# Weight splits inside the gate's slices, and rotation tables made one layer ahead

## What is computed

```python
# first block, per layer
proj = rms_norm(h, g_mix) @ w_in            # q, k, v, xr, gr
o = diff_attention(partial_rope(q), partial_rope(k), v, lam)   # 4 heads, causal
y = rg_lru(causal_conv(xr)) * gelu(gr)
h = h + concat([o, y]) @ w_out
h = h + square(relu(rms_norm(h, g_mlp) @ w_mlp_in)) @ w_mlp_out
gate = sigmoid(rms_norm(h, g_ple) @ w_ple_gate)
h = h + gate * (p @ w_ple_proj)
# second block, per layer
h = rms_norm(x, g_pre_mix)
u, q, k, v, iq, ik, iw = split(h @ w_in)    # q, k, iq, ik are rotated (rope)
mix = concat([pool_mixer(u), top128_attention(q, k, v, iq, ik, iw)]) @ w_out
x = x + rms_norm(mix, g_post_mix)
x = x + rms_norm(square(relu(rms_norm(x, g_pre_ffn) @ w_ff1)) @ w_ff2, g_post_ffn)
```

## Time and profile before

| | before |
|---|---|
| time, 3 runs: median (lowest, highest) | 2562.69 (2561.21, 2563.07) |
| the profiled execution's own time | 2563.96 |
| its span | 2561.9 |
| TensorE busy | 2422.1 (95%) |
| VectorE / ScalarE / GpSimd busy | 1474.0 / 833.4 / 360.5 |
| mean granted clock of TensorE | 0.975 |

### The profile page before, as it was taken

How to read it: one execution, slowest core, us unless ns; L and a number is a source line. 1 busy time by engine, 2 the same in 40 slices (tenths; PEclk the granted TensorE clock), 3 DMA queues, 4 the chain that set the end, 5 groups by cost and what they waited for, 6 DMA issues and landing times.

```text
span 2561.9 us, 28886 instructions
## 1 busy us (share of the span) xinstructions
PE 2422.1 (95%) x11342; PEld 1942.7 (76%) x11350; DVE 1474.0 (58%) x2112; ACT 833.4 (33%) x1166; POOL 360.5 (14%) x281
## 2 busy tenths in 40 slices
PE   7999999999998999999897989999989888999996
PEld 6877888887786888888766767888866666788885
DVE  6765554455776644444669756435556965634543
ACT  4554222234546322223431443222232244322221
POOL 2002000001100100001227321000033632200002
PEclk9999999999999999999999989999989999999998
DMA  4311222222221222222211111222212111122221
GB/s 151 108 62 54 104 95 97 98 99 81 98 92 50 83 99 99 98 99 97 77 66 66 50 66 66 93 105 98 82 66 91 66 50 66 50 98 99 98 98 49
DMA packets 33017, 215.53 MB, mean 84 GB/s; under 512 B 4112, under 2 KB 4368, under 8 KB 7824
## 3 DMA queue, kind: packets, MB, share of 16 engines
q1 hardware_dynamic: 32912, 214.08, 23.3%
HBM read 211.97 MB, written 2.10 MB: 84 GB/s over the span
## 4 chain that ended last, share of the span: by engine, by line
PE 81%; DVE 10%; POOL 4%; ACT 3%; issue 2%; DMA 0%; POOLq 0%; ACTq 0%; SPq 0%; DVEq 0%
PE ps L356 74%; DVE wl L328 1%; ACT wh L321 1%; POOL wl L337 1%; DVE tmp L1792 1%; DVE hl L509 1%; POOL arena L1446 1%; PE ps L1921 1%; PE ps L1957 1%; PE ps L1981 1%; PE ps L1971 1%; PE ps L469 1%; PE ps L1191 1%; PE ps L493 1%; DVE gl L509 1%
## 5 line engine op out<-in xcount | busy, mean ns | idle before, releaser
L356 PE MATMUL ps<-gh,wh 128*128 128x512 f32 x1504 | 602.1, 400 | 39.0 <-DVE gl L509 15.5
L356 PE MATMUL ps<-hh,wh 128*128 128x512 f32 x1504 | 602.5, 401 | 32.4 <-issue 13.2
L356 PE MATMUL ps<-gh,wl 128*128 128x512 f32 x1504 | 591.0, 393 | 0.0
L356 PE MATMUL ps<-hh,wl 128*128 128x512 f32 x1504 | 590.8, 393 | 0.0
L356 PE MATMUL ps<-gl,wh 128*128 128x512 f32 x1504 | 590.8, 393 | 0.0
L356 PE MATMUL ps<-hl,wh 128*128 128x512 f32 x1504 | 590.7, 393 | 0.0
L328 DVE TENSOR_TENSOR wl<-wr,wh 128x2048 fp32r<-128x2048 f32 x176 | 406.2, 2308 | 275.1 <-ACT wh L321 275.1
L321 ACT ACTIVATE wh<-wr 128x2048 fp32r<-128x2048 f32 x196 | 374.1, 1909 | 553.9 <-PE ps L356 553.9
L356 PEld LDWEIGHTS ps<-gh,wh 128*128 128x128 f32 x1504 | 285.1, 190 | 112.9 <-issue 21.9
L356 PEld LDWEIGHTS ps<-hh,wh 128*128 128x128 f32 x1504 | 285.0, 190 | 109.3 <-issue 29.3
L356 PEld LDWEIGHTS ps<-hh,wl 128*128 128x128 f32 x1504 | 284.6, 189 | 61.8
(11 more groups left out here) (232 smaller groups left out, 2385.7 us busy)
## 6 DMA issues: line engine op xcount, KB each, us to landing
wr<-in_weights SPq DMA_DIRECT2D x196, 1024.0 KB, 4.8
x<-in_xt SPq DMA_DIRECT2D x4, 512.0 KB, 7.0
out_yt<-x SPq DMA_DIRECT2D x8, 256.0 KB, 2.0
tmp<-in_positions SPq DMA_DIRECT2D x4, 256.0 KB, 2.7
arena<-in_gates SPq DMA_DIRECT2D x2, 512.0 KB, 8.0
arena<-in_embed SPq DMA_DIRECT2D x2, 512.0 KB, 5.6
par<-in_params_b SPq DMA_DIRECT2D x2, 274.0 KB, 3.0
par<-in_params_a SPq DMA_DIRECT2D x2, 157.5 KB, 6.7
```

The costliest lines, as they stand in the source:

```text
L356: done = pe.matmul(out, stationary, moving, start=(first and n == 0), stop=(last and n == 2), skip_group_check=True)
```

## The change

1. In the gate tail of both first-stack layers the splits of the next chunks move from ahead of a pair of slices to inside a slice: on ScalarE behind the sigmoid of slice 0, 3 and 5, on VectorE behind the addition to x of the same slice.
2. The tables of both second-stack layers are made in the layer before. SP loads the positions into the arena once the sixteenth score of that layer's attention is out, ahead of the MLP's weight loads. VectorE makes the angles between the first and the second half of the last MLP block. ScalarE takes the sines behind that half's first chunk. The layer itself reads the finished tables and writes the products with its root to the old place.
3. In the second-stack layers the mask copy moves from the layer's start to the end of the top-128 search.

```diff
+SPLIT_AFTER_GATE = {0: A_GATE + 2, 3: A_GATE + 3}
+FOLLOWING_AFTER_GATE = 5
+NEXT_ANGLES, NEXT_TABLES = 2048, 3072
+def load_next_positions(sp, mem, sem, positions, steps):
+    sp.wait_ge(sem["scored"], steps)
+    sp.dma_start(mem.arena[:, NEXT_ANGLES:NEXT_ANGLES + S].bitcast(I32), positions).then_inc(sem["next_positioned"], 16)
+def next_angles(dve, steps, mem, sem):
+    dve.wait_ge(sem["next_positioned"], 16)
+    rotary_angles(dve, steps, mem, mem.arena[:, NEXT_ANGLES:NEXT_ANGLES + S], mem.arena[:, NEXT_ANGLES + S:NEXT_ANGLES + 2 * S])\
+        .then_inc(sem["next_tables"], 1)
+def next_sines(act, mem, sem):
+    whole, left = mem.arena[:, NEXT_ANGLES:NEXT_ANGLES + S], mem.arena[:, NEXT_ANGLES + S:NEXT_ANGLES + 2 * S]
+    act.wait_ge(sem["next_tables"], 1)
+    act.activation(mem.next_sin, left, ACT.Sin, scale=mem.cst[:, C_SIGN:C_SIGN + 1]).then_inc(sem["next_tables"], 1)
+    act.activation(mem.next_cos, whole, ACT.Sin, scale=-1.0, bias=mem.cst[:, C_HPI:C_HPI + 1]).then_inc(sem["next_tables"], 1)
...
 first stack, SP:
+        if following.second:
+            load_next_positions(sp, mem, sem, next_positions, STEPS)
         with sp.Fori(0, FB) as j:
...
 first stack, ScalarE:
             for t in range(2):
                 own_slice(2, 2 * (c - c0 - BC) + t, A_TILE[c] + t, par[:, AP_GPLE:AP_GPLE + KT])
+            if following.second and c == c0 + BC:
+                next_sines(act, mem, sem)
...
         for c in range(A_GATE, A_CHUNKS):
-            if c + 1 < A_CHUNKS:
-                if c > A_GATE:
-                    split_high(act, mem, sem, c + 1, a_used(c + 1))
-            else:
-                split_high(act, following.mem, following.sem, 0)
             for t in range(2):
                 n = 2 * (c - A_GATE) + t
                 act.wait_ge(sem["drained"], A_TILE[c] + t + 1)
                 act.activation(tmp[:, 1, :], tmp[:, 0, :], ACT.Sigmoid).then_inc(sem["gate_out"], 1)
+                if n in SPLIT_AFTER_GATE:
+                    split_high(act, mem, sem, SPLIT_AFTER_GATE[n], a_used(SPLIT_AFTER_GATE[n]))
+                if n == FOLLOWING_AFTER_GATE:
+                    split_high(act, following.mem, following.sem, 0)
                 act.wait_ge(sem["finished"], n + 1)
                 input_high(act, following, n)
...
 first stack, VectorE:
         mlp_first(c0, once, FB - 1)
+        if following.second:
+            next_angles(dve, own, mem, sem)
         for c in range(c0 + BC, A_GATE):
             split_low(dve, mem, sem, c + 1)
...
                 dve.tensor_tensor(x[:, n, :], x[:, n, :], tmp[:, 1, :], ALU.add).then_inc(sem["finished"], 1)
+                if n in SPLIT_AFTER_GATE:
+                    split_low(dve, mem, sem, SPLIT_AFTER_GATE[n])
+                if n == FOLLOWING_AFTER_GATE:
+                    split_low(dve, following.mem, following.sem, 0)
...
 second stack, SP (and the same load ahead of the MLP if a layer follows):
-        sp.dma_start(tmp[:, 0, :].bitcast(I32), positions).then_inc(sem["positioned"], 16)
...
 second stack, ScalarE:
-        act.wait_ge(sem["tables"], 1)
-        act.activation(sin, tmp[:, 1, :], ACT.Sin, scale=cst[:, C_SIGN:C_SIGN + 1]).then_inc(sem["turned_tables"], 1)
-        act.activation(cos, tmp[:, 0, :], ACT.Sin, scale=-1.0, bias=cst[:, C_HPI:C_HPI + 1]).then_inc(sem["turned_tables"], 1)
         split_high(act, mem, sem, 2, b_used(2))
...
         for c in range(c0 + BC, B_CHUNKS):
+            if following and c == c0 + BC + 1:
+                next_sines(act, mem, sem)
...
 second stack, VectorE:
-        dve.wait_ge(sem["positioned"], 16)
-        rotary_angles(dve, own, mem, tmp[:, 0, :], tmp[:, 1, :]).then_inc(sem["tables"], 1)
-        own.mark(dve.tensor_copy(mask[0], cst[:, C_CHUNK:C_CHUNK + P]))
...
-        dve.wait_ge(sem["turned_tables"], 2)
-        own.mark(dve.tensor_tensor(sin, sin, mem.rb[:, :], ALU.mult))
-        own.mark(dve.tensor_tensor(cos, cos, mem.rb[:, :], ALU.mult))
+        dve.wait_ge(stage.before.sem["next_tables"], 3)
+        own.mark(dve.tensor_tensor(sin, mem.next_sin, mem.rb[:, :], ALU.mult))
+        own.mark(dve.tensor_tensor(cos, mem.next_cos, mem.rb[:, :], ALU.mult))
...
         picks(TOPK // 8 - rounds[0])
+        own.mark(dve.tensor_copy(mask[0], cst[:, C_CHUNK:C_CHUNK + P]))
...
         mlp_first(B_CHUNKS - 2 * BC, once, FB - 1)
+        if following:
+            next_angles(dve, own, mem, sem)
         mlp_second(B_CHUNKS - 2 * BC, once)
```

More of the change, by code:

```diff
@@ L124, in __init__ @@
         self.praw = arena[:, A1_CR:A1_CR + 2 * S]
+        self.next_cos, self.next_sin = (arena[:, NEXT_TABLES + S * n:NEXT_TABLES + S * (n + 1)] for n in range(2))
 def build(nc, weights, params_a, params_b, gains, gates, embed, constants, positions, xt, out):
@@ L152, in build @@
             if n < DEPTH:
-                programs.append(first_stack_layer(stage, n, weights, params_a, gains, gates, embed, constants, xt, positions[0:P, :]))
+                programs.append(first_stack_layer(stage, n, weights, params_a, gains, gates, embed, constants, xt,
+                                                  positions[0:P, :], positions[P:2 * P, :]))
             else:
@@ L191 @@
     "o_mean o_root o_normed o_back o_high o_low embed_high embed_low hidden hidden_high hidden_low gate_in gate_out padded "
-    "finished "
+    "finished next_positioned next_tables "
 )
 B_NAMES = (
-    "loaded0 loaded1 next_gains vectors positioned high low product drained squared gathered summed mean root diag spread "
-    "kept gain_high gain_low own tables turned_tables weights_turned masked swapped rotated logit rectified weighed "
+    "loaded0 loaded1 next_gains vectors high low product drained squared gathered summed mean root diag spread "
+    "kept gain_high gain_low own weights_turned masked swapped rotated logit rectified weighed "
     "pooled_ready pool_product pool_high pool_low scored maxed exped scaled_done turned untangled weighted pair_high pair_low "
     "updated branch_scaled added zeroed hidden hidden_high hidden_low padded pool_own finished folded raw_squared "
-    "raw_gathered raw_summed raw_mean raw_root raw_diag raw_spread raw_kept renewed "
+    "raw_gathered raw_summed raw_mean raw_root raw_diag raw_spread raw_kept renewed next_positioned next_tables "
 )
@@ L585, in a_used, with first_stack_layer @@
     return A_TILE[c - 1]
-def first_stack_layer(stage, layer, weights, params, gains, gates, embed, constants, xt, positions):
+NEXT_ANGLES, NEXT_TABLES = 2048, 3072
[11 more added lines that the diff above has]
+    act.activation(mem.next_cos, whole, ACT.Sin, scale=-1.0, bias=mem.cst[:, C_HPI:C_HPI + 1]).then_inc(sem["next_tables"], 1)
+def first_stack_layer(stage, layer, weights, params, gains, gates, embed, constants, xt, positions, next_positions):
     mem, sem, following, shared = stage.mem, stage.sem, stage.following, stage.shared
@@ L1132, in program_dve @@
         for c in range(A_GATE, A_CHUNKS):
-            if c + 1 < A_CHUNKS:
-                if c > A_GATE:
-                    split_low(dve, mem, sem, c + 1)
-            else:
-                split_low(dve, following.mem, following.sem, 0)
             for t in range(2):
@@ L1398, in program_sp @@
             load_gains(sp, mem, sem, gains, DEPTH + layer + 1)
+            load_next_positions(sp, mem, sem, positions, STEPS)
         with sp.Fori(0, FB) as j:
```

## The result

The changed kernel takes 2543.28 us (median of 4 runs, 2541.06 to 2544.82); the kernel before, run beside it on the same chip, took 2561.95 (4 runs, 2559.49 to 2563.07). The ratio is 0.9932, 95% interval 0.992 to 0.9945: 0.7% faster. A later set of runs of the changed kernel gave 2539.86 and 0.9926 (0.9914 to 0.9937). The profiled execution has a span of 2539.9 us at a mean granted clock of 0.979; before it was 2561.9 at 0.975.

A forecast was written before the change was run, and what follows sets the result against it. TensorE, busy 95% of the span, bounds the kernel, losing time to gate-tail and second-stack stalls and low clock. 4.5 + 8.4 − 0.3 + 4.9 = 17.5 us saved gives 2545.2 us, range 2541 to 2554.

The forecast's parts named there:

- Gate of layer 0, 4.5: Layer 0's gate tail: third chunk's split comes in time, saving 2.8 us of stall and 1.6 to 1.7 of clock.
- Gate of layer 1, 8.4: Layer 1's gate tail: ScalarE-VectorE-GpSimd chain walked slice by slice, about 1 us per GpSimd delay; second stack's second chunk 8.4 us earlier.
- rival 2: Layer 1's gate: no GpSimd delay, tail saves 10.3, low clock behind first sums (1.6) goes; total 21.0, 2541.7 us; chance 0.12.
- Rival 1: Gate tail: each GpSimd pair holds VectorE for all its 2.6 us; total saved 10, time 2552.7 us; chance 0.16.
- the lost clock behind the 4.1 us stall included: Layer 1's gate: the 8.4 us saved was said to contain the clock lost behind the 4.1 us stall.
- MLP tail, -0.3: Layer 1's last MLP block: added angle work delays the weight split, so TensorE waits 0.3 us; ends 0 and 2.5 for sines.
- Second stack, first layer, 0: Start of the second stack's first layer: the tables give TensorE nothing; the 1.09 us drained-bank wait stays.
- Second layer, 3.3 + 1.6: Second stack's second layer start: drained bank 3.3 us earlier, plus 1.6 us of low clock counted as saved (ends 0 and 1.6).
- Rival 3: Tables give 0.5 us: second layer keeps its low clock, MLP tail stalls 0.3 and 2.5; total 13.4, 2549.3 us; chance 0.10.
- Rival 4: MLP starts: weight loads starve behind SP's new wait, making the kernel slower, 2575 us at 35 us lateness; chance 0.03.
- VectorE adds of 1.5 us and more in most slices: Sign for layer 1's gate: VectorE's adds would take 1.5 us or more in most slices.
- the drained bank's wait: Sign at the start of the second stack's second layer: TensorE's 2.71 us wait for the drained bank falls to near 1.3.

The follow-up runs named there:

- experiment 4: Changed kernel with the third gate chunk's split put back to its old place, behind slice 1, in layer 0 alone; 2547.4 us, once.
- experiment 5: Changed kernel with GpSimd's second addition of each pair in the gate cut to 8 columns; 2539.22 us, ratio 0.9914 to the kernel before.
- Experiment 7: Changed kernel with the angle work done twice in the MLP tail of the first stack's last layer; 2548.06 us, once.
- experiment 8: Changed kernel with the folded layer's weight split ahead of its spread, and layer 1's angles behind the next weight split, sines one chunk later; 2539.14 us, ratio 0.9913.
- experiment 1: Kernel before with only the gate tail's splits moved, tables made in the layer itself as before; 2544.6 us, ratio 0.994.
- experiment 3: The changed kernel again, unaltered, timed beside the kernel before; 2539.86 us, ratio 0.9926.
- experiment 6: Changed kernel with the fourth gate chunk's split one slice earlier, behind slice 2's sigmoid, in both layers; 2539.73 us, ratio 0.9918.
- experiment 9: Changed kernel with the fourth gate chunk's split one slice earlier, the folded layer's split ahead of its spread, and angles and sines later; 2539.14 us, ratio 0.9918.
- experiment 2: Changed kernel with the old gate order, so only the tables' half of the change; 2557.39 us, ratio 0.9987 to the kernel before.

## Why the prediction was right, and where it was not

The forecast was 2545.2, 17.5 us saved. The ratio of 0.9932 on 2562 is 17.4 us (14.1 to 20.5), the second set's 0.9926 is 19.0 (16.1 to 22.0). The mechanism was right for the order of the work and wrong in part for the clock. That the total agrees to 0.1 us with the first set is luck: the terms below miss by 0.9 up to 1.6 down, and the clock gave on average some us that no term has. By its own steps:

- **Gate of layer 0, 4.5.** Right: experiment 4 gives 4.50, with its 2.8 us of stall and the clock back at 0.86. Missed was the chunk of the next layer, 0.86 more. The prediction looked only at whether that split would be in time after the change, not at the 0.56 that it had cost before.
- **Gate of layer 1, 8.4.** The walk held: from the first sigmoid to the second stack's second split 41.7 us (1216.22 to 1257.94) where 41.1 was predicted, brackets of 0.79 and 0.64 where 0.8 and 0.7 were. The second chunk starts 49.41 us behind the root copy (1262.72 less 1213.31), where it was 57.06 (1277.59 less 1220.53): 7.65 saved. Of the 0.75 too much, 0.6 is in the chain itself: by ScalarE's rows the two slices in which GpSimd's pair falls on the multiply took 5.30 and 5.28 where 5.1 was taken, and the other steps are each 0.1 or less over. The rest is TensorE's way from the last k-slice to the second chunk, 4.98 where 4.9 was taken, and rounding. GpSimd's delay was the right term: experiment 5 takes the second additions out, and what rival 2 says of the order then happens (no bracket, sums 2.5 us earlier; the prediction has 10.3 less 8.4, 1.9, for it). Rival 2's other half, the low clock behind the first sums, came in the first profile of after and stayed away in the second (60.37 and 58.76 in the table). Rival 1's full 2.6 us per pair did not come; the last section shows why.
- **The clock in layer 1's gate.** One part of my reasoning was wrong without changing the sum: "the lost clock behind the 4.1 us stall included". The two profiles of before have a granted clock of 0.57 and of 0.79 from 1234 to 1242. The run with the higher clock got through the chunk sooner, waited 0.92 for the next one instead, and both came to the second stack's first chunk 42.57 us behind the root copy (1263.10 less 1220.53, 1262.04 less 1219.47). What the one run lost more by the low clock cost it nothing, since the chain, not TensorE, set the pace.
- **MLP tail, -0.3.** The sign and place right, the size 0.42, the slower restart included. Experiment 7 shows that there is no cover. The relus behind a sigmoid cost nothing, since no other stretch grew.
- **Second stack, first layer, 0.** Right: 0.79 and 1.07 stay (in the changed kernel at 1274.43 and 1279.39), and experiment 8 shows what they wait for.
- **Second layer, 3.3 + 1.6.** The order of the work gave 3.83: from the chunk before (1919.62, with its bracket of 0.18) to the one behind the drained bank it was 19.57, and is 15.74 (1904.65 to 1920.39). Of the 0.5 more, 0.2 lies ahead of the multiplication of the sine by the root (now at 1917.48) and 0.3 behind it, in the rotation, where the 3.3 had assumed no change. The weak step is the clock: "I count the 1.6 as saved". Of the three profiles that have the 2.7 bracket, two have a low clock behind it (0.86 and 0.75 in 12 us) and one has 1.00; of the ten with 0.81 none has a low clock there. So the 1.6 is no fixed part of the wait's price, and the tables alone did not lower the clock's loss on average (below).

By the order of the work the change is worth 5.36 + 7.65 - 0.42 + 3.83 = 16.4 us (with the 1.7 of clock in layer 0's gate, which came every time). That is 1.1 less than the forecast: 0.9 and 0.5 more than the terms for layer 0 and the second layer, 0.75 and 0.1 less for layer 1's gate and MLP, and 1.6 less for the clock. The first pair of profiles shows 22.0. The rest is the clock, 1.6 in layer 1's attention and 3.2 in the second stack's second attention (5.09 less the 1.9 of the drained bank), and 0.6 ahead of the first root copy, which comes at 38.66 and 38.03 (and at 38.80 in the second profile of after, so that this too differs from run to run).

Whether the new order also loses less to the clock can be read from the granted clock that is on record for every run. The share of the clock that was not granted, times the span, averaged over the runs of a kernel (all of one set; the standard deviation over a kernel's runs is 4 to 7 us):

| kernel | runs | mean time | span times share not granted |
|---|---|---|---|
| before | 16 | 2560.0 | 56.0 |
| gate edit alone | 6 | 2545.0 | 49.6 |
| tables alone | 11 | 2557.0 | 56.9 |
| after | 6 | 2540.8 | 49.1 |

Over the three sets, 32 runs of the kernel before average 56.7, and 30 runs of the six kernels with the new gate order (experiments 1, 3, 5, 6, 8 and 9) average 48.7. The gate edit lowers the loss, the tables don't. Part of the 8 us is known: 1.7 is layer 0's gate, already in the 5.36, and 1.7 to 3.4 was lost behind the 4.10, where it cost no time. What is left shows in the mean times. They are 2.0 us better than the 12.95 for the gate edit, and 2.8 better than the 16.4 for the changed kernel; by the same estimate experiments 5, 6, 8 and 9 are 2.7 to 4.7 better than their order of the work says, and the tables alone are 0.5 worse. So low-clock stretches also came less often with the new gate order, worth some 2 to 5 us for which the prediction had no term. By what steps, so far behind the gate, no run here shows.

Rival 3 (the tables give 0.5 us) lies just outside experiment 2's interval of 1.0 to 5.9, and the sixth line of the table and the 0.42 in the MLP tail, where it has 2.8, speak against it. Rival 4 (weight loads starve) is refuted by MLP stretches that changed by nothing but the 0.42. Among the signs, the "VectorE adds of 1.5 us and more in most slices" came in four of eight, and the drained bank's wait is 0.81 where 1.3 was forecast.

## What to carry to other kernels

Where three engines in turn work on each slice, walk their chain from end to end before counting TensorE's brackets one by one: it tells whether a bracket is a loss of its own or only the place where a slow chain is waited for. Moving one split then shifts the bracket, and only work taken off the chain (here GpSimd's additions) shortens it. And take a second profile of the kernel before, before you put a price on a low-clock stretch: only one that comes every time may stand at its full price. For the others, average the granted clock over many runs of both kernels; a profile of each can't tell.

## What the runs showed of the hardware

**The clock.** Two runs of the same kernel before differ at the same work: in layer 1's attention the granted clock is 0.65 from 832 to 836 in one and 1.00 in the other, and the stretch takes 210.92 and 209.34; the second stack's second attention takes 239.39 and 234.87. Its first attention took 235.06 to 239.60 us over the eleven profiles of kernels that do the same work there but for one mask copy of 0.2 us. Low stretches are at the 1.2 GHz level (0.50). Of the low stretches priced here only the one behind the 2.60 bracket of layer 0 came every time, in all four profiles that have this bracket (layer 0's gate 59.79, 59.78, 59.80 and 58.93 us). The Trainium skill ("TensorE: Matmul & The Clock Gate", section "Part 1: The HAM clock gate") says that the gate looks at activity in windows that run on by themselves, whatever the kernel does. Low stretches that come and go behind equal waits agree with that; no run here shows the windows themselves.

**GpSimd and VectorE.** Both were slowed when they met, and in a pattern: the one that came second. GpSimd's second add at 1226.37 comes under VectorE's multiply of 1226.15 (to 1226.95). In the kernel before, the same add took 1.26 while VectorE stood idle:

```profile
1232.05 1.26 POOL L1418 TENSOR_TENSOR arena<-arena 128x512 f32<-128x512 f32 x1
```

1.26 from 1226.95 on would end at 1228.21, and it ends at 1228.10. VectorE's next add, which starts at 1226.99, meets this one; 0.69 of a free add from 1228.10 on would end at 1228.79, and it ends at 1228.65. The multiply at 1237.44 meets the one of 1236.91 to 1238.66, and ends 0.55 behind it (1239.21). GpSimd's first add at 1234.97 comes under VectorE's split of 1233.53 (to 1235.81) and takes 2.00; a free 1.34 (its row at 1230.01) from 1235.81 on would end at 1237.15, and it ends at 1236.97. So what a meeting costs is what is left of the instruction that was first, here about 1 us, and not the 2.6 us of a pair. The Trainium skill ("SBUF — State Buffer", section "SBUF: two separate sides") says just this of a VectorE instruction with two inputs in SBUF and a GpSimd instruction that reads SBUF: whichever is first keeps the shared port pair for its whole instruction, and the other blocks until then. The rows agree to 0.2 us. The prediction read the rule as if it held VectorE for a whole pair, and left 0.9 us of saving by it; read rightly it asks for about 1 us per meeting, as in the 8.4.
